# Running a projection's first vector burst and three of its four banks ahead of the last quarter of the low-rank sums

## The reference, cut to what matters

```python
mod = (cs @ W['ada_w'][l] + W['ada_b'][l]).reshape(B, N_MOD, D)      # cs = silu(c), two rows
h = modulate(rmsnorm(x, W['norm_mix_g'][l]), mod[:, 0], mod[:, 1])
xx = concatenate([h_prev[:, None, :], h[:, :-1, :]], axis=1) - h
r = (h + xx * mu[0]) @ p['wr']
w = ... tanh((h + xx * mu[1]) @ p['w1']) @ p['w2'] ...               # 2048 x 96
a = sigmoid(p['a0'] + ((h + xx * mu[4]) @ p['a1']) @ p['a2'])        # 2048 x 96
g = sigmoid((h + xx * mu[5]) @ p['g1']) @ p['g2']                    # 2048 x 256
```

## Time and profile before

| | |
|---|---|
| median of three executions | 3276.63 us (3274.47, 3276.63, 3277.03) |
| span of the profiled execution, first to last instruction | 3276.5 us |
| TensorE (PE) busy | 3178.9 us, 97% |
| VectorE (DVE) busy | 2072.3 us, 63% |
| ScalarE (ACT) busy | 1377.6 us, 42% |
| mean granted TensorE clock | 0.995 |

### The profile page before, as it was taken

How to read it: one execution, slowest core, us unless ns; L and a number is a source line. 1 busy time by engine, 2 the same in 40 slices (tenths; PEclk the granted TensorE clock), 3 DMA queues, 4 the chain that set the end, 5 groups by cost and what they waited for, 6 DMA issues and landing times. The chain is left out here.

```text
span 3276.5 us, 81582 instructions
## 1 busy us (share of the span) xinstructions
PE 3178.9 (97%) x32100; PEld 2978.9 (91%) x32100; DVE 2072.3 (63%) x3570; ACT 1377.6 (42%) x2180; POOL 129.3 (4%) x245
## 2 busy tenths in 40 slices
PE   7899998998999999999999999999999999999998
PEld 3699987777889999999999889998999999999998
DVE  4544536776468778778788866555578865444455
ACT  2333425665353334333343654334454334343342
POOL 0000000110000000000000000000000000000000
PEclk9999999999999999999999999999999999999999
DMA  9878750001878888888777433442456755455453
GB/s 395 307 274 295 274 188 21 22 22 55 337 259 306 306 296 304 306 298 306 264 242 255 155 118 97 137 140 92 142 191 228 252 175 167 163 164 166 161 167 119
DMA packets 182923, 668.87 MB, mean 204 GB/s; under 512 B 21367, under 2 KB 21537, under 8 KB 182209
## 3 DMA queue, kind: packets, MB, share of 16 engines
q1 hardware_dynamic: 155808, 570.49, 49.2%
q0 software_dynamic: 26912, 95.47, 8.9%
HBM read 661.79 MB, written 4.09 MB: 203 GB/s over the span
## 5 line engine op out<-in xcount | busy, mean ns | idle before, releaser
L714 ACT ACTIVATE sb_whi<-sb_raw 128x1024 fp32r<-128x1024 f32 x778 | 811.5, 1057 | 1099.8 <-PE ps L2003 790.8
L1134 DVE TENSOR_TENSOR sb_wlo<-sb_raw,sb_whi 128x1024 fp32r<-128x1024 f32 x778 | 943.2, 1222 | 518.2 <-ACT sb_whi L714 516.5
L2003 PE MATMUL ps<-sb_ah,sb_whi 128*128 128x288 f32 x2688 | 468.0, 296 | 4.7 <-DVE sb_al L1340 2.5
L2003 PE MATMUL ps<-sb_ah,sb_wlo 128*128 128x288 f32 x2688 | 465.4, 295 | 0.0
L2003 PE MATMUL ps<-sb_al,sb_whi 128*128 128x288 f32 x2688 | 465.1, 294 | 0.0
L2003 PEld LDWEIGHTS ps<-sb_ah,sb_whi 128*128 128x128 f32 x2688 | 391.6, 188 | 14.3 <-issue 13.4
L2003 PEld LDWEIGHTS ps<-sb_al,sb_whi 128*128 128x128 f32 x2688 | 393.2, 188 | 0.0
L2003 PEld LDWEIGHTS ps<-sb_ah,sb_wlo 128*128 128x128 f32 x2688 | 393.1, 188 | 0.0
L1972 PE MATMUL ps<-sb_ah,sb_whi 128*128 128x288 f32 x1040 | 313.6, 302 | 8.2 <-DVE sb_al L1340 4.5
L1973 PE MATMUL ps<-sb_ah,sb_wlo 128*128 128x288 f32 x1040 | 307.5, 296 | 0.0
L1974 PE MATMUL ps<-sb_al,sb_whi 128*128 128x288 f32 x1040 | 306.9, 295 | 0.0
(11 more groups left out here) (326 smaller groups left out, 4553.2 us busy)
## 6 DMA issues: line engine op xcount, KB each, us to landing
sb_raw<-stream SPq DMA_DIRECT2D x1070, 512.0 KB, 4.5
sb_strip<-strips POOLq DMA_DIRECT2D x156, 512.0 KB, 5.0
sb_crow<-crow POOLq DMA_DIRECT2D x8, 512.0 KB, 5.2
sb_x<-xT SPq DMA_DIRECT2D x1, 2304.0 KB, 16.1
sb_x<-xT POOLq DMA_DIRECT2D x1, 2304.0 KB, 10.2
yT<-sb_x SPq DMA_DIRECT2D x4, 576.0 KB, 2.8
sb_lwa<-lw POOLq DMA_DIRECT2D x16, 130.0 KB, 2.4
sb_lwg<-lw POOLq DMA_DIRECT2D x16, 130.0 KB, 2.4
```

What stands on the lines that cost most here:

```text
L714: nc.scalar.activation(whi[:, q % SPL, :], raw[:, n, :], ACT.Copy).then_inc(hi_ready, 1)
L1134: nc.vector.tensor_tensor(wlo[:, q % SPL, :], raw[:, n, :], whi[:, q % SPL, :], ALU.subtract).then_inc(lo_ready, 1)
L2003: ins = mm(PS[:, m, 0:T], w[:, n % SPL, a:a + P], z[:, 2 * p + j, :], start=False, stop=False)
```

## The change

The low-rank sums move from banks 0, 1, 2, 3 to banks 5, 6, 7, 3. The column sums of groups 0 to 7 of the vector product move from bank 5 to columns 256 to 263 of bank 4, and TensorE then waits before the next group's first matmul in bank 4 until VectorE has read them. TensorE now does, before `low_rank(3)`: r's first vector burst, and the matmuls of r's slots 0 and 1 that go to banks 0, 1 and 2. After `low_rank(3)` it does the matmuls of these slots for bank 3, and goes on with slot 2. The splits of slots 0 and 1 move up on ScalarE and VectorE, into the last quarter. In block 15 the gate product comes first, so that its weights, and with them places 2 and 3 of `whi` and `wlo`, are free a little earlier. The amount of arithmetic is the same.

```diff
--- before.py
+++ after.py
@@ -53,6 +53,7 @@
 PER_QUARTER = 16
 MIXES = 7
 LEVELS = 6
+LOW_BANKS = (5, 6, 7, 3)
 DEC = float(np.exp(-0.5))
 
 
@@ -806,19 +807,25 @@
             act.wait_ge(set_up, 3)
             norm_root(N_MIX0, x)
             for quarter in range(4):
+                if quarter == 3:
+                    split(BY["r"], 0)
                 for b in range(4 * quarter, 4 * quarter + 4):
                     modulate(N_MIX0, b, True)
+                if quarter == 3:
+                    split(BY["r"], 1)
                 for b in range(4 * quarter, 4 * quarter + 4):
                     mix_high(0, b)
-            for j in range(BY["r"].hoist):
-                split(BY["r"], j)
-
-            act.wait_ge(mix_used, 3 * KB)
-            for z in range(4):
-                m = 96 if z < 2 else P
-                nc.scalar.activation(mids[0:m, z, :], PS[0:m, z, 0:T], ACT.Copy).then_inc(mids_done, 1)
 
             def r_pair(p):
+                if p == 0:
+                    act.wait_ge(mix_used, 3 * KB // 2)
+                if p == 1:
+                    act.wait_ge(mix_used, 3 * KB - 2)
+                    for z in (3, 2, 0, 1):
+                        if z < 2:
+                            act.wait_ge(mix_used, 3 * KB - 1 + z)
+                        m = 96 if z < 2 else P
+                        nc.scalar.activation(mids[0:m, z, :], PS[0:m, LOW_BANKS[z], 0:T], ACT.Copy).then_inc(mids_done, 1)
                 if p == 3:
                     act.wait_ge(mids_done, 4)
                     nc.scalar.activation(mids[0:96, 0, :], mids[0:96, 0, :], ACT.Tanh).then_inc(mids_done, 1)
@@ -1149,8 +1156,9 @@
 
                 b = 4 * g if place is None else place
                 dve.wait_ge(ada_fin, g + 1)
+                sums = PS[:, 5, 0:8] if place is None else PS[:, 4, 256:264]
                 nc.vector.tensor_tensor(mod[:, bass.ds(b, 4), :],
-                                        PS[:, 5, 0:8].rearrange("p (a t) -> p a t", a=4),
+                                        sums.rearrange("p (a t) -> p a t", a=4),
                                         vec[:, bass.ds(b + ADAB, 4)].rearrange("p (a t) -> p a t", t=1).to_broadcast([P, 4, 2]),
                                         ALU.add).then_inc(mod_ready, 1)
 
@@ -1418,12 +1426,16 @@
                 nc.vector.tensor_tensor(x[:, b, :], x[:, b, :], work[:, 6, :], ALU.mult).then_inc(scaled, 1)
             for i in range(4):
                 quarter = range(4 * i, 4 * i + 4)
+                if i == 3:
+                    split(BY["r"], 0)
                 for b in quarter:
                     change(b)
                     ch.wait()
                     if b % 4 < 2:
                         for c in range(3):
                             low_rank_mix(b, c)
+                if i == 3:
+                    split(BY["r"], 1)
                 if i < 3:
                     vectors_group(2 * i + 2)
                 for b in quarter[2:]:
@@ -1443,10 +1455,12 @@
             ch.inc(nc.vector.tensor_copy(last[:, 0, :], hb[:, :, TP:TP + 1].rearrange("p a t -> p (a t)")))
             ch.wait()
             nc.vector.tensor_copy(last[:, 1, :], hb[:, :, T:T + 1].rearrange("p a t -> p (a t)")).then_inc(last_ready, 1)
-            for j in range(BY["r"].hoist):
-                split(BY["r"], j)
+
+            def gates_read(p):
+                if p == 0:
+                    dve.wait_ge(mix_used, 3 * KB - 2)
             k_pair, v_pair = mix_pair(1, 2, "r"), mix_pair(2, 3, "k")
-            gemm("r", "k", lambda p: None, early=first_two(k_pair))
+            gemm("r", "k", gates_read, early=first_two(k_pair))
             gemm("k", "v", but_two(k_pair), early=first_two(v_pair))
             gemm("v", None, but_two(v_pair))
 
@@ -1930,6 +1944,9 @@
                 if p == 0 and not first:
 
                     pe.wait_ge(arow_ready, s.ada0 + it)
+                    if isinstance(it, int) and s.ada0 + it <= 8:
+
+                        pe.wait_ge(mod_ready, s.ada0 + it)
                 for j in range(2):
                     for z in range(2):
                         g, a = 64 * j + 32 * z, 512 * j + 256 * z
@@ -1962,8 +1979,9 @@
                 pe.wait_ge(arow_ready, g + 1)
                 if not first:
                     pe.wait_ge(mod_ready, g)
+                sums = PS[:, 4, 256:264] if isinstance(g, int) and g < 8 else PS[:, 5, 0:8]
                 for m in range(2):
-                    ins = mm(PS[:, 5, 4 * m:4 * m + 4], arow[:, P * m:P * m + P], con[:, SEL:SEL + 4],
+                    ins = mm(sums[:, 4 * m:4 * m + 4], arow[:, P * m:P * m + P], con[:, SEL:SEL + 4],
                              start=True, stop=True)
                 ins.then_inc(ada_fin, 1)
 
@@ -2016,13 +2034,24 @@
                         ins.then_inc(gemm_done, 1)
                 ins.then_inc(slot_used, 1)
 
+            def part_slot(s, p, banks):
+
+                pe.wait_ge(lo_ready, s.q0 + p + 1)
+                pe.wait_ge(a_ready, s.a0 + 2 * p + 2)
+                for m in banks:
+                    for j in range(2):
+                        a = 512 * j + P * m
+                        ins = three(PS[:, m, 0:T], whi[:, s.q0 + p, a:a + P], wlo[:, s.q0 + p, a:a + P],
+                                    ah[:, 2 * p + j, 0:T], al[:, 2 * p + j, 0:T], p == 0 and j == 0, False)
+                return ins
+
             def gemm(name):
                 s = BY[name]
                 xh, xl = (ah, al) if s.src == "A" else (bh, bl)
 
-                def group(it):
+                def group(it, begun=0):
                     half = s.mixed and halved(s, it)
-                    for p in range(8):
+                    for p in range(begun, 8):
                         if half and p == 0:
                             for a in range(BURST):
                                 half_slot(s, it, a)
@@ -2041,7 +2070,7 @@
                         ada_finish(s.ada0 + it)
                 if name in ("r", "m1_0_0", "m1_1_0"):
 
-                    group(0)
+                    group(0, 2 if name == "r" else 0)
                     rounds(pe, 1, 4, group)
                 else:
                     rounds(pe, 0, 4, group)
@@ -2087,12 +2116,13 @@
                 pe.wait_ge(lora1_in, 64)
                 for b in [4 * quarter + z for z in blocks]:
                     gates = l1g[b // (KB // 2)][:, b % (KB // 2), :]
-                    for i, w in enumerate((l1w[:, b, :], l1a[:, b, :], gates)):
+                    for i in (2, 0, 1) if b == KB - 1 else range(3):
+                        w = (l1w[:, b, :], l1a[:, b, :], gates)[i]
                         q = 3 * b + i
                         pe.wait_ge(mix_ready, PER_QUARTER * quarter + 3 * (b % 4) + i + 1)
                         m = 96 if i < 2 else P
                         for z in range(2 if i == 2 else 1):
-                            ins = mm(PS[0:m, i + z, 0:T], w[:, P * z:P * z + m], mx[:, q % MIXES, :],
+                            ins = mm(PS[0:m, LOW_BANKS[i + z], 0:T], w[:, P * z:P * z + m], mx[:, q % MIXES, :],
                                      start=b == 0, stop=b == KB - 1)
                         ins.then_inc(mix_used, 1)
             vectors_group(1)
@@ -2106,10 +2136,17 @@
                 low_rank(i, (2, 3))
                 half_group(2 * i + 3, 1)
                 ada_finish(2 * i + 3)
+            s = BY["r"]
+            for a in range(BURST):
+                ada_slot(s, 0, a)
+            for p in range(2):
+                part_slot(s, p, range(3))
             low_rank(3)
-
-
-            pe.wait_ge(mids_done, 4)
+            pe.wait_ge(mids_done, 1)
+            for p in range(2):
+                part_slot(s, p, (3,)).then_inc(slot_used, 1)
+
+
             gemm("r")
             gemm("k")
             gemm("v")
```

## The result

The change made the kernel slower: a median of 3287.06 us (8 runs) against 3276.92 (8 runs of the kernel before), a ratio of 1.0028, 95% interval 1.0018 to 1.0037, or 5.9 to 12.1 us. One of the eight, at 4399.81 us, was disturbed and isn't in the ratio; without it the median is 3286.55. The profiled execution is the first of the eight: 3287.57 us, of which the span is 3286.0.

What follows compares the result with a forecast made beforehand. It took TensorE, busy 97% of the span, to bound the kernel. Late loads, 5.3 us, plus one clock fall, 1.6, made 6.9 us on the profiled span of 3276.5, 0.1 under the median: 3283.5 us, range 3278.0 to 3285.9.

Steps and rivals of the forecast that it cites:

- the late burst: r's second vector burst, before slot 4: SyncE's loads issued late, so TensorE goes on 4.6 to 5.8 us late, 5.3 taken.
- The clock: TensorE's granted clock: one fall to 1.2 GHz after the new 4.1 us gap, 1.6 us, bounds 0 and 1.7.
- the sum: Total loss: 5.3 us for late loads plus 1.6 for one clock fall, 6.9 us; nothing later gives it back.
- The bank moves: Column sums in bank 4 make TensorE wait for VectorE's reading; covered by the load stream, 0 us taken.
- The wait: ScalarE's first split waits for `raw[4]` until 110.5, so the last quarter's modulations start 4.4 us late.
- 4.1 us idle ahead of slot 1: TensorE finishes slot 0's part at 115.3, then idles 4.1 us until VectorE's second split is done at 119.4.
- a rival (0.20): A second clock fall among the waits of r's second burst: up to 1.7 us more, 3285.2 us; chance 0.20.
- my 9.7 to 10.9: Microseconds from SyncE's issue of `raw[7]` at 132.4 to the landing of the last load of r's second burst.
- my 5.3: TensorE's lateness in microseconds after r's second burst, chosen from 4.6 to 5.8 because its loads land late.
- one constant: After the opening, each row of r, k and v is late by the same amount, through to the end.
- 0.4 us ahead of its use: In the kernel before, the second burst's last load landed at 135.8, read as leaving no slack.

Runs made afterwards that it cites:

- e5: The kernel before with only the bank moves and TensorE's new wait, its own order everywhere: 3275.20 us against 3275.24, ratio 1.0000.
- e4: The kernel before with only ScalarE's first split put ahead of the last quarter's modulations: 3279.85 us against 3277.65, ratio 1.0008.
- e1: The changed kernel with SyncE issuing the four vector slots ahead of the four product slots in r's first round: 3281.50 us, ratio 1.0014 to before.
- e6: The changed kernel with filler matmuls, never read, where TensorE would wait: 3285.75 us, ratio 1.0030 to the kernel before.
- e11: The changed kernel with filler matmuls where TensorE would wait, measured once more: 3286.05 us, ratio 1.0026 to the kernel before.
- e10: The changed kernel with no further edit, measured once more: 3287.39 us against 3276.16 for the kernel before, ratio 1.0035.
- e12: The kernel before with no edit, measured against itself: 3278.32 us against 3276.87, ratio 1.0004.

## Why the prediction was wrong

I forecast 3283.5 us, with 3285.9 as the upper end; 3287.06 was measured. The direction and the late burst were right. The clock was sized too small, and a rest of the loss lies outside the opening, where the sum had nothing.

**Right, and to the tenth.** ScalarE waits until 110.6 (110.5 by the sum), modulates from 111.60 (111.6); `sb_xx` from 112.87 (112.85); split 1 at 118.19 (118.2). The bank moves cost nothing (the trace of e5). The wait by itself is real (the trace of e4), and so is the late burst (e1).

**Right, but the row looked otherwise.** I forecast 4.1 us idle ahead of slot 1, and 2.28 is there: slot 0's part ran at half clock and so filled the gap. The sum of gap and slow work ends at the same split, 119.4.

**The step that failed: "The clock".** It took one fall on the path, 1.6 us, with 1.7 as its upper bound, and left a second to a rival (0.20). TensorE ran 10.2 us at half clock between 113 and 148 in both traces of the change, three times what the one fall of before lasted. The opening lost 8.69 us where the sum had 6.9. By its links: `raw[7]` was issued at 134.26, not 132.4 (1.9: the fall ahead of the low-rank sums delays them, and with them this issue); the loads took 10.8 us from there, of my 9.7 to 10.9, and my 5.3 stood for 10.4 (0.4); the last slot at half clock took 0.96 us to slot 4 where I had 0.5 (0.5); slot 4 itself ran slow for a moment more (0.6). 5.3 + 1.9 + 0.4 + 0.5 + 0.6 = 8.7, where the sum was 5.3 + 1.6. Held against e6 and e11, the 5.3 for the loads was about right (5.1 and 5.5 by the estimate), and the clock cost some 3 us, not 1.6.

The three falls did not cost alike. The first, from 113.4, cost the path nothing: slot 0's part ended at 117.2 and TensorE then waited 2.28 us for split 1 in any case. The second, from 120.2, is the one that the sum booked: slot 1's part took 3.9 us (119.47 to 123.40) where I had 2.4, which is 1.5 of the 1.9. The third, from 144.1, I had left out: it is the 0.5 and the 0.6. Where a fall lies is partly luck: the trace of e1, the same program as far as TensorE's slot 2 but for SyncE's order, ran slot 1's part at full clock.

The Trainium skill (TensorE: Matmul & The Clock Gate, HAM oscillation) tells of a kernel in which the wait for a load behind each short piece of work, some 3 to 5 us long, throttled TensorE before every next piece. The waits here are shorter, and the traces show both outcomes. In the change a fall came behind 3.00 us, one behind 2.28, and one behind the burst's waits of 1.05, 1.59 and 0.65. e10 has the burst's waits (1.75 and three of 0.65) and no fall behind them.

**What the opening leaves over.** The opening's 8.7 us alone would have given 3285.3, inside the range. The sum said that nothing later changes the loss, and that each later row is late by one constant. It is not one constant (8.7 us up to 450 us, 12.3 at 1290, 9.5 at the end), and the measured loss is larger than the opening's: 9.2 us by the ratio (5.9 to 12.1) and 11.5 by e10's (6.9 to 16.1), 10.1 and 11.2 by the medians. The reason that the sum gave, TensorE busy throughout, was read from 300 to 400 us; in the trace of before it is busy 54.49 of the 60 us from 640 to 700.

Two places of this rest can be named. At 830 us the change ran 6.8 us at half clock where before ran 3.4 at 820, and at 1878 before had a fall of 3.4 us and the change none; e10 is like the change in both. Within the change's executions the slower ones have the lower mean clock: 0.994 at 3283.45 us, 0.991 at 3289.47. So a part of the rest may be the clock again, which is not shown. The 0.5 to 2.8 us that lie between the opening's loss and the whole stay open: equal kernels differ by as much (e12, e5), and one trace can't tell.

One reading was wrong without bearing on the sum. The last load of before's burst landed at 135.8, and I called that 0.4 us ahead of its use. The burst begins at 136.19, but its last slot is used some 1.4 us later, so there were some 1.8 us of slack.

## What to carry to other kernels

On an engine that works strictly in program order, an operation whose data comes by a load must stand behind the work that others wait for, and not only behind what it needs itself: one split moved ahead of eight modulations made them 4.3 us late. When work is moved on the engine that sets the pace, follow the queue that feeds it to the next use: SyncE's in-order loads cost more here (5.6 us) than all idle time that the move was to fill (5.0), and issuing them in the order of use was two lines. Where a change leaves gaps ahead of work on the path, count a possible fall of the clock for each, as a range, and let it delay the loads that hang on that work too. And before a trace explains a median, look where the traced execution stands among the others.

## What was not expected of the hardware

The same kernel split its time at half clock differently from one execution to the next (in the opening, three stretches of 3.4 us in the change, one of 10.2 in e10), for the same total. Idle stretches of nearly one length were followed by a fall and not: 2.30 us was not in before, 2.28 us was in the change. And a stretch with the same instructions, the 3125 us behind the opening, took up to 4.7 us less in another execution (e5 and e12 against before), about half of what this change costs.
